# Reordering the middle of a streaming-encoder step and its routing list

## The chip, the cores and the metric

The kernel runs on one core of one Trainium2 chip. The metric is the device time of one execution, in microseconds (us); the median of several runs is quoted. PE is the matrix engine, DVE the vector engine, ACT the scalar engine, POOL the general one, SP the engine that only issues DMAs.

## The reference, cut to what matters

One layer is applied to a prompt of 512 tokens and to a sample of 64 tokens with a past of 512. In the kernel they are five row tiles: t = 0 to 3 of 128 rows, and t = 4 of 64.

```
z = rmsnorm(x) @ w_in                       # G, R, U, K, V, Q column blocks
o_gla, S = gla_recurrence(q, k, v, log_a, s0)     # 4 heads, chunks of 64
o_pool   = pool_mixer(u, hist)              # windows 2, 4, 8, 16
o_diff   = softmax(q0 k0') v - lam * softmax(q1 k1') v    # 4 heads, two maps
x += concat(o_gla, o_pool, o_diff) @ w_out
x += memory_attend(rmsnorm(x), mk, mv)      # mk, mv = rmsnorm(mem) @ w_mem_kv
x += sum over the 2 chosen of 16 experts of gate * (silu(h w_g) * (h w_u)) w_d
y  = rmsnorm(x)
```

## The kernel before, in words

**Order.** Each engine has its own instruction list, written out by hand, and engines meet only at semaphores. PSUM banks are handed out by plans: `PJ` (from `projection_plan`, two banks for projections), `TR` (transposes, two banks) and `SC` (scores, two halves). A plan gives each use its rank, its reader (A for ACT, V for DVE) and its bank; `claim` makes PE wait until the bank's previous user has been read.

**Split products.** Projections are in single precision made of two rounded parts. A weight unit of 128x2048 is loaded by SP (`dense_load`) into a ring of four (`DRING`), rounded by ACT (`w_high`) and its rest formed by DVE (`w_low`); a unit with a norm gain takes four instructions of 512 columns on each, a w_out unit one. A projection of a full tile with K = 1024 is 24 matmuls of 512 columns (hi*hi, lo*hi, hi*lo); of tile 4, whose two parts are packed, 16. Units 8, 9 are V, 10, 11 Q, 12, 13 memk, 14, 15 memv, 16 to 19 w_out. A load into a slot waits until tile 4 (or memory tile 1) of the unit four places back is projected.

**The middle.** PE projects blocks G, R, U, K and all five tiles of V, turns the decayed keys (`kend`), forms the chunk states (`kv`), projects Q0 and Q1, and runs five gated-attention tiles (`gla_scores`, `gla_out`), after which it projects Q2, Q3, Q4, memk0 and memk1 in turn; the pool products (`pool_map`) stand behind tiles 3 and 4. Then come the 20 steps s of differential attention (tile t = s // 4, head h = s % 4): PE does scores of step s + 1, waits for `pd_ready` of s, transposes the probabilities, and multiplies them by V. DVE forms row maxima (`row_max`) and normalises; ACT does the exponentials (`exps`). A filler stands in each step: a half (12 matmuls) of memv0 or memv1 in tile 0, of w_out of tile t - 1 afterwards. POOL splits units 16 and 17.

**Routing.** Behind the memory stage the x2 rows are transposed, `router` gives logits, DVE picks groups and experts (L1733 to L1757), `("pos",)` counts positions, and `placed` (one-hot of position) times `held` (entry by expert) gives the list `idx_sb` (L1784). Then DVE works out the overflow list (L1788 to L1810), and splits the first expert's gate weights (`split_lo(0, 0, 0)` and `(0, 0, 1)`). POOL gathers rows by the list (L741). Sixteen experts follow; in the last one DVE's order is `split_lo`, `hidden`, `hid_lo`.

## Time and profile before

| what | us |
|---|---|
| runs (3) | 838.66, 848.07, 848.48; median 848.07 |
| the profiled execution | 847.1 |
| its span, first to last instruction | 845.4 |
| mean granted PE clock over the span | 0.914 |

The profiled execution stands 1.0 us below the median and 1.7 us above its own span. Clock is in shares of full speed; a matmul row's duration overlaps its neighbours', so rates are read from the starts. [idle <-releaser] behind a row is the time that the engine stood before it and whose instruction ended that.

### The profile page before, as it was taken

The page shows a single profiled execution, that of the slowest core. Times are in us where ns is not written, and L with a number is a line of the kernel's source. Part 1 is how long each engine was busy: PE and PEld are TensorE (multiplying, and loading weights), DVE is VectorE, ACT ScalarE, POOL GpSimd, SP SyncE. Part 2 cuts the span into 40 slices and gives each one's busy share as a digit, 9 for nine tenths or more (in the row PEclk, how much of TensorE's full clock was granted, in tenths as well). Part 3 has the DMA queues.
Part 4 walks back from the last instruction along what each step waited for, and adds up shares of the span by engine and source line. Part 5 has one row for each costly group of instructions (what it writes and reads, how often), then busy time and mean ns, then how long its engine had stood idle before and what let it go on. Part 6 is the DMA issues. An engine that isn't in the chain of part 4 may idle for free.

```text
span 845.4 us, 9688 instructions
## 1 busy us (share of the span) xinstructions
PE 722.8 (86%) x3454; PEld 574.9 (68%) x3454; DVE 526.2 (62%) x660; ACT 416.5 (49%) x584; POOL 153.3 (18%) x171
## 2 busy tenths in 40 slices
PE   4979988998688898978898956999999999999920
PEld 3778876775465656657786854888888888888720
DVE  4533624563635445535644565898888898988817
ACT  5445433233233323333532322877788778788612
POOL 4102910011700101000001011121112321112004
PEclk9999999999599889889998756999999999999975
DMA  9323133123352000013005154899999999999346
GB/s 335 121 90 124 76 130 143 54 99 112 125 221 104 0 1 1 1 50 125 1 26 224 34 228 146 336 358 373 388 375 380 391 377 381 382 387 385 147 159 215
DMA packets 31631, 160.67 MB, mean 190 GB/s; under 512 B 5598, under 2 KB 5932, under 8 KB 16748
## 3 DMA queue, kind: packets, MB, share of 16 engines
q1 hardware_dynamic: 22224, 138.20, 42.8%
q10 hardware_dynamic: 4604, 12.26, 4.0%
q0 software_dynamic: 4768, 9.73, 3.1%
q8 instruction: 22, 0.36, 0.2%
q14 instruction: 13, 0.11, 0.0%
HBM read 150.90 MB, written 16.62 MB: 198 GB/s over the span
## 4 chain that ended last, share of the span: by engine, by line
PE 63%; DVE 15%; issue 10%; ACT 9%; DMA 3%; ACTq 0%; POOL 0%; SPq 0%; DVEq 0%; POOLq 0%
PE pj L1898 40%; PE scores L1898 15%; ACT wh L810 3%; PE tr_a L1906 3%; PE tr_v L1898 2%; DVE wl L1292 2%; PE tr_v L1906 1%; DVE w_lo L1320 1%; PE tr_a L2274 1%; DMA raw<-in_dense 1%; DVE hid L1292 1%; DMA yg<-y_rows 1%; DVE w_lo L1292 1%; ACT y L1217 1%; PE scores L2251 1%
## 5 line engine op out<-in xcount | busy, mean ns | idle before, releaser
L1292 DVE TENSOR_TENSOR wl<-moe_raw,wh 128x2048 fp32r<-128x2048 f32 x96 | 217.5, 2289 | 40.9 <-ACT wh L810 40.7
L810 ACT ACTIVATE wh<-moe_raw 128x2048 fp32r<-128x2048 f32 x96 | 182.4, 1920 | 35.6 <-PE scores L1898 12.0
L1898 PE MATMUL pj<-w_hi,xT_hi 128*128 128x512 f32 (+2 forms) x192 | 72.2, 376 | 11.7 <-DVE w_lo L1320 10.4
L685 POOL TENSOR_SCALAR rs<-stat 128x1 f32<-128x1 f32 (+4 forms) x31 | 11.4, 369 | 387.5 <-ACT sq_scr L823 202.0
L1898 PE MATMUL pj<-w_hi,xT_lo 128*128 128x512 f32 (+2 forms) x192 | 70.2, 365 | 0.0
L1898 PE MATMUL pj<-w_lo,xT_hi 128*128 128x512 f32 (+2 forms) x192 | 70.1, 365 | 0.0
L1320 DVE SCALAR_TENSOR_TENSOR w_lo<-raw,pack_a,w_hi 128x512 fp32r<-128x512 f32 (+2 forms) x64 | 44.8, 760 | 36.9 <-ACT w_hi L855 36.9
L746 POOL DMA_INDIRECT y_rows<-y,idx_sb x16 | 16.1, 1004 | 235.9 <-ACT y L1217 235.9
L1898 PE MATMUL pj<-wh,xgh 128*128 128x512 f32 x128 | 52.2, 408 | 2.8 <-DVE xgl L1292 2.8
L870 ACT ACTIVATE pdT<-tr_a 128x256 f32<-128x256 f32 (+4 forms) x24 | 9.4, 392 | 86.7 <-PE tr_a L1906 86.7
L1898 PE MATMUL scores<-wh,hTh 128*128 128x512 f32 x128 | 49.9, 390 | 1.4 <-DVE hTl L1292 1.4
L1898 PE MATMUL tr_v<-wh,xgh 128*128 128x512 f32 x128 | 51.1, 399 | 0.0
L1898 PE MATMUL pj<-wh,xgl 128*128 128x512 f32 x128 | 50.5, 394 | 0.0
L1898 PE MATMUL pj<-wl,xgh 128*128 128x512 f32 x128 | 50.4, 394 | 0.0
L1898 PEld LDWEIGHTS pj<-w_hi,xT_hi 128*128 128x128 f32 x192 | 37.7, 196 | 18.3 <-POOL ext L669 9.0
L1898 PE MATMUL tr_v<-wh,xgl 128*128 128x512 f32 x128 | 49.9, 390 | 0.0
L1898 PE MATMUL tr_v<-wl,xgh 128*128 128x512 f32 x128 | 49.9, 390 | 0.0
L1898 PE MATMUL scores<-wh,hTl 128*128 128x512 f32 x128 | 49.9, 390 | 0.0
L1898 PE MATMUL scores<-wl,hTh 128*128 128x512 f32 x128 | 49.8, 389 | 0.0
L741 POOL DMA_INDIRECT xg<-h_rows,idx_sb x16 | 41.7, 2604 | 16.3 <-DVE idx_sb L1784 7.5
L1898 PEld LDWEIGHTS pj<-w_hi,xT_lo 128*128 128x128 f32 x192 | 37.7, 196 | 5.5
L866 ACT ACTIVATE rowbuf<-pj,rs 128x512 f32<-128x512 f32 (+1 forms) x22 | 13.4, 607 | 56.9 <-PE pj L1898 56.9
(366 smaller groups left out, 1597.9 us busy)
## 6 DMA issues: line engine op xcount, KB each, us to landing
moe_raw<-in_w_exp_gate SPq DMA_DIRECT2D x32, 1024.0 KB, 7.3
moe_raw<-in_w_exp_up SPq DMA_DIRECT2D x32, 1024.0 KB, 7.3
moe_raw<-in_w_exp_down SPq DMA_DIRECT2D x32, 1024.0 KB, 8.2
raw<-in_dense SPq DMA_DIRECT2D x17, 1024.0 KB, 6.9
yg<-y_rows SPq DMA_DIRECT2D x4, 1024.0 KB, 9.4
xT_raw<-in_xT SPq DMA_DIRECT2D x4, 512.0 KB, 11.7
x_rows<-in_x_prompt SPq DMA_DIRECT2D x4, 512.0 KB, 12.3
xw<-in_x_prompt ACTq DMA_DIRECT2D x1, 2048.0 KB, 8.3
```

The source lines that it names most:

```text
L685: link(pool.tensor_scalar(rs[rows, n, cs], stat[rows, n, cs], EPS, None, ALU.add))
L741: pool.indirect_dma_start(xg[:, b, :], None, h3_rows, bass.IndirectOffsetOnAxis(ap=idx, axis=0), bounds_check=TOK - 1, oob_is_err=False).t ...
L746: pool.indirect_dma_start(y_rows, bass.IndirectOffsetOnAxis(ap=idx, axis=0), y[:, b, :], None, bounds_check=2 * TOK - 1, oob_is_err=False) ...
L810: act.activation(wh[s4][:, :], moe_raw[:, SLOT_OF[s6], :], ACT.Copy).then_inc(hi_done, 1)
L866: return act.activation(dst, src, ACT.Copy, scale=scale)
L870: act.activation(dst, src, ACT.Copy).then_inc(tr_act, 1)
L1217: act.activation(y[:, b, 512 * c:512 * c + 512], py[c], ACT.Copy).then_inc(y_done, 1)
L1292: return dve.tensor_tensor(out, a, b, op)
L1320: dve.scalar_tensor_tensor(out=w_lo[:, n % DRING, w * k:w * k + w], in0=srcs[k], scalar=gains[:, GAIN_OF[name], r // P + k:r // P + k + 1] ...
L1898: return pe.matmul(out, lhsT, rhs, start=start, stop=stop, skip_group_check=True)
L1906: ins = pe.transpose(bank[0:n, c0:c0 + r], src, ident[0:r, 0:r])
L2251: ins = pe.transpose(px[g][:, P * k:P * k + P], xg[:, buf, P * (4 * g + k):P * (4 * g + k) + P], ident[:, :])
```

## The change

In the middle only V0 is projected ahead of `kend`, V1 after `kv`, and V2, V3, V4, Q0 and Q1 stand behind the gated-attention tiles. Q2, Q3, Q4, memk0, memk1, memv0, memv1, three pool products and the four w_out projections of tiles 0 and 1 become fillers of steps 0 to 11, each split into a part ahead of the wait for `pd_ready` and a part behind the transposes. Projections that are fillers all use bank 1 and `diff_o` always bank 0. Splits of units 13 to 19 stand in steps 0 and 3 to 8 (`LATE_SPLIT`), all on ACT and DVE; POOL splits nothing. The memory transpose's split is in step 1. ACT does `exps` of the next step directly behind the copy of the transposes. For the list, `held` and `placed` are bf16 (four values of small size for each entry instead of two), the splits of the first expert's units stand elsewhere, the overflow list is worked out ahead of the last expert, `x2_T(4)` is ahead of `router(3)`, and one more Silu of one element stands behind the routing exponentials. In the diff eight columns of deep indentation are left off.

```diff
 def projection_plan():
-    plan = [((b, t), row_reader(t)) for b, _, _ in IN_BLOCKS[:-1] for t in range(TILES)] + [(("Q", t), "A") for t in range(2)]
+    plan = [((b, t), row_reader(t)) for b, _, _ in IN_BLOCKS[:-2] for t in range(TILES)] + [(("V", t), "A") for t in range(2)]
     for t in range(TILES):
         plan += [(("gla_o", t), "V")]
-        plan += [(("Q", t + 2), row_reader(t + 2))] if t + 2 < TILES else [(("memk", t - 3), "A")]
-        plan += [(key, "V") for key in POOL_USES[2 * t - 6:2 * t - 4]] if t >= 3 else []
-    for t in range(TILES):
-        plan += [(("w_out", c, t - 1), "V", 1 - t % 2) for c in range(2)] if t else [(("memv", i), "A", 1) for i in range(2)]
-        plan += [(("diff_o", t), "V", t % 2)]
+        plan += [(("V", t + 2), row_reader(t + 2))] if t + 2 < TILES else [(("Q", t - 3), "A")]
+    plan += [(("Q", t), row_reader(t), 1) for t in range(2, TILES)] + [(("memk", 0), "A", 1), (("diff_o", 0), "V", 0)]
+    plan += [(("memk", 1), "A", 1), (("memv", 0), "A", 1), (("memv", 1), "A", 1)]
+    plan += [(key, "V", 1) for key in POOL_USES[0:3]] + [(("diff_o", 1), "V", 0), (POOL_USES[3], "V", 1)]
+    for t in range(2, TILES):
+        plan += [(("w_out", c, u), "V", 1) for u in ((0, 1) if t == 2 else (t - 1,)) for c in range(2)]
...
 HIGH = {key: n for n, key in enumerate(high_plan())}
...
-WO_SPLIT = (5, 6)
+LATE_SPLIT = {0: 13, 3: 14, 4: 15, 5: 16, 6: 17, 7: 18, 8: 19}
...
-    sp.wait_ge(pj_full, PJ[("Q", 1)][0] + 1)
...
     sp.wait_ge(states_ready, 1)
...
+    for n in range(MK_UNIT, MV_UNIT):
+        dense_load(n)
+    sp.wait_ge(pj_full, PJ[("Q", 1)][0] + 1)
+    sp.dma_start(memT_raw[:, :, :], A["memT"]).then_inc(memT_in, 16)
     for n in range(MV_UNIT, MQ_UNIT):
         dense_load(n)
     sp.dma_start(mq_raw0[:, :], unit(MQ_UNIT)).then_inc(mq_in[0], 16)
...
     for t in range(TILES):
         root(("gla", t))
-    for n in (WO_UNIT, WO_UNIT + 1):
-        pool.wait_ge(unit_in[n % DRING], 16 * (n // DRING + (n % DRING > 0)))
...
-            c = slice(512 * k, 512 * k + 512)
-            link(pool.tensor_copy(w_hi[:, n % DRING, c], raw[:, n % DRING, c]))
-            pool.tensor_tensor(w_lo[:, n % DRING, c], raw[:, n % DRING, c], w_hi[:, n % DRING, c].bitcast(F32),
-                               ALU.subtract).then_inc(wo_done, 1)
...
-            act.activation(memT_hi[:, :, :], memT_raw[:, :, :], ACT.Copy).then_inc(memT_hi_done, 1)
         if t + 2 < TILES:
-            rows_block("Q", t + 2, ROW_AT[("Q", t + 2)])
...
+        if t == 4:
+            kq_out("Q", 0)
+        if t >= 3:
+            rows_block("Q", t - 3, ROW_AT[("Q", t - 3)])
         if t:
             mixg_high(t - 1)
-        if t >= 3:
-            mem_out("memk", t - 3)
-            for n in range(2 * t - 6, 2 * t - 4):
-                pool_high(n)
-        if t == 4:
-            mk_out(0)
-            w_high(MV_UNIT)
+    w_high(MK_UNIT)
...
+            exps(s + 1)
+        if s < 2:
+            rows_block("Q", s + 2, ROW_AT[("Q", s + 2)])
+        if s in (3, 4):
+            mem_out("memk", s - 3)
...
+        if s in (5, 6):
+            mem_out("memv", s - 5)
+        if s == 6:
+            pool_high(0)
+        if s == 7:
+            pool_high(1)
+            pool_high(2)
         if h == 1 and t:
             mixd_high(t - 1)
-        if s + 1 < len(STEPS):
-            exps(s + 1)
         if s == 0:
-            w_high(MV_UNIT + 1)
             act.wait_ge(state_out, 16 * 8)
             act.dma_start(xw[:, 0:4, :], A["x_prompt"][0].rearrange("(t p) n -> p t n", p=P)).then_inc(x_again, 16)
             act.dma_start(xw[0:DEC, 4, :], A["x_sample"][0]).then_inc(x_again, 16)
-        if t == 0 and h % 2 == 1:
-            mem_out("memv", h // 2)
-        if s in WO_SPLIT:
-            w_high(WO_UNIT + 2 + WO_SPLIT.index(s))
-        if h == 1 and t >= 2:
-            x1_square(t - 2)
+        if s == 1:
+            act.wait_ge(memT_in, 16)
+            act.activation(memT_hi[:, :, :], memT_raw[:, :, :], ACT.Copy).then_inc(memT_hi_done, 1)
+        if s in LATE_SPLIT and s != 7:
+            w_high(LATE_SPLIT[s])
         if h == HEADS - 1:
             act.wait_ge(pj_full, PJ[("diff_o", t)][0] + 1)
             act.wait_ge(ms_dve, TILES + t)
...
+            if t >= 2:
+                x1_square(t - 2)
+        if s == 7:
+            pool_high(3)
+            w_high(LATE_SPLIT[s])
...
     for i, v in enumerate((r20[1], r5[3])):
         act.wait_ge(route_arg, i + 1)
         act.activation(v, v, ACT.Exp).then_inc(route_exp, 1)
+    act.activation(small[0:1, 1:2], neghalf[0:1, 0:1], ACT.Silu)
...
     mixg_low(TILES - 1)
+    w_low(MK_UNIT)
     for s, (t, h) in enumerate(STEPS):
         r, nk, b = ROWS[t], keys_of(t), s % 2
+        if s == 9:
+            dve.wait_ge(x_again, 32)
+        if 9 <= s <= 12:
+            add_rows("w_out", (s - 9) % 2, (s - 9) // 2, xw, xw)
         sc_read(dve, last_score(t, h))
         link(dve.reciprocal(recip[0:r, b, :], psum_[0:r, b, :]))
         link(tt(recip[0:r, b, 1:2], recip[0:r, b, 1:2], lams[0:r, 5:6], ALU.mult))
         link(dve.tensor_scalar(prob[0:r, b, 1, 0:nk], prob[0:r, b, 1, 0:nk], recip[0:r, b, 1:2], None, ALU.mult))
...
             row_max(s + 1)
-        if s == 0:
-            w_low(MV_UNIT + 1)
+        if s == 1:
+            dve.wait_ge(memT_hi_done, 1)
+            tt(memT_lo[:, :, :], memT_raw[:, :, :], memT_hi[:, :, :].bitcast(F32), ALU.subtract)\
+                .then_inc(memT_lo_done, 1)
+        if s == 2:
+            fold_rows("Q")
+        if s == 6:
+            pool_low(0)
+        if s == 7:
+            pool_low(1)
+            pool_low(2)
         if h == 1 and t:
             mixd_low(t - 1)
-        if s in WO_SPLIT:
-            w_low(WO_UNIT + 2 + WO_SPLIT.index(s))
         if h == 0 and t:
             diff_norm(t - 1)
+        if s in LATE_SPLIT and s != 7:
+            w_low(LATE_SPLIT[s])
         if h == HEADS - 1:
-            if t:
...
     link(dve.tensor_reduce(r5[4], r20[1], AX.X, ALU.add))
     link(dve.reciprocal(r5[4], r5[4]))
...
-        link(dve.scalar_tensor_tensor(out=more, in0=cnt, scalar=float(P * q), in1=more, op0=ALU.is_gt, op1=ALU.add))
-    link(dve.memset(ones16, 1.0))
-    link(dve.tensor_tensor_scan(upto, ones16, more, 0.0, ALU.mult, ALU.add))
...
+    link(dve.tensor_scalar(listed, parts[:, 0], -64.0, float(EMPTY), ALU.mult, ALU.add))
+    tt(idx_sb[:, :, :].rearrange("p e v -> p v e"), listed, parts[:, 1], ALU.subtract).then_inc(pj_dve, 1)
+    split_lo(0, 0, 0)
+    split_lo(0, 0, 1)
     def x_lo(e, b):
         for g in range(2):
...
+    link(dve.tensor_scalar(more, cnt, float(P), None, ALU.is_gt))
+    for q in range(2, 5):
+        link(dve.scalar_tensor_tensor(out=more, in0=cnt, scalar=float(P * q), in1=more, op0=ALU.is_gt, op1=ALU.add))
+    link(dve.memset(ones16, 1.0))
+    link(dve.tensor_tensor_scan(upto, ones16, more, 0.0, ALU.mult, ALU.add))
...
+    link(dve.tensor_reduce(extra_f, r8x16, AX.X, ALU.add))
+    link(dve.tensor_copy(extra_i[:, 0:MAX_EXTRA], extra_f))
+    dve.tensor_copy(extra_i[:, MAX_EXTRA:MAX_EXTRA + 1], upto[0:1, E - 1:E]).then_inc(list_ready, 1)
     step(E - 1, 1, last=True)
     dve.wait_ge(list_ready, 1)
...
-            rows_T("Q", t + 1, 4)
-        else:
-            mk_T(0)
+            value(t + 2)
+        if t == 3:
+            query(0)
+        if t == 4:
+            rows_T("Q", 0, 4)
+            query(1)
+            tr_read(pe, ("K", 4))
+            tr_read(pe, ("Q", 0))
+            diff_scores(0)
         if t:
...
-            pe.wait_ge(poolw_in, 16)
-        if t >= 3:
-            for n in range(2 * t - 6, 2 * t - 4):
-                pool_map(n)
     mixg_T(TILES - 1)
-    tr_read(pe, ("K", 4))
-    tr_read(pe, ("Q", 4))
+    rows_T("Q", 1, 4)
     pj_read(pe, ("V", 3))
     pj_read(pe, ("V", 4))
-    mk_T(1)
+    def filler(s, part):
+        if s < 3:
+            query(s + 2, part)
+        elif s < 5:
+            mem_kv("memk", s - 3, part)
+        elif s < 7:
+            mem_kv("memv", s - 5, part)
+        elif s == 7:
+            pool_map(1 + part)
+        elif s < 12:
+            w_out((s - 8) % 2, (s - 8) // 2, part)
     for s, (t, h) in enumerate(STEPS):
         r, nb, b = ROWS[t], key_blocks(t), s % 2
         if s + 1 < len(STEPS):
+            if h == HEADS - 1:
+                tr_read(pe, ("Q", t + 1))
             diff_scores(s + 1)
+        if late_rows(s):
+            kind, i = late_rows(s)
+            rows_T(kind, i, 4) if kind == "Q" else mk_T(i)
+        filler(s, 0)
         pe.wait_ge(pd_ready, s + 1)
...
             transposes(("pd", t, h, 1), [(0, prob[0:r, b, 0, PAST:PAST + DEC])])
+        filler(s, 1)
         if h == 1 and t:
             mixd_T(t - 1)
-        if h >= 2:
-            if t:
-                w_out(1, t - 1, h - 2)
-            else:
-                mem_kv("memv", 1, h - 2)
+        if h >= 2 and t >= 3:
+            w_out(1, t - 1, h - 2)
         if h == 0:
             j = claim("pj", PJ, PJ_KEYS, ("diff_o", t), pj_act, pj_dve)
         tr_read(pe, ("pd", t, h, 0))
...
-        if h < 2:
-            if t:
-                w_out(0, t - 1, h)
-            else:
-                mem_kv("memv", 0, h)
+        if s == 6:
+            pe.wait_ge(pool_ready, 4)
+            pe.wait_ge(poolw_in, 16)
+            pool_map(0)
+        if s == 7:
+            pool_map(3)
+        if h < 2 and t >= 3:
+            w_out(0, t - 1, h)
     w_out(0, TILES - 1, 0)
     def x1_T(t):
...
     x2_T(TILES - 2)
     router(2)
+    x2_T(TILES - 1)
     router(3)
-    x2_T(TILES - 1)
     router(4)
...
-            ins = mm(pj[j][:, 0:2 * E], placed[0:r, i, t, :], held[0:r, i, t].rearrange("p v e -> p (v e)"),
+            ins = mm(pj[j][:, 0:4 * E], placed[0:r, i, t, :], held[0:r, i, t].rearrange("p v e -> p (v e)"),
                      i == 0 and t == 0, i == 1 and t == TILES - 1)
```

## Rows read from the trace of the kernel before
**Rows 1.** The page, part 1: busy time of each engine.
```profile
PE 722.8 (86%) x3454; PEld 574.9 (68%) x3454; DVE 526.2 (62%) x660; ACT 416.5 (49%) x584; POOL 153.3 (18%) x171
```
**Rows 2.** Windows: stretch, busy us by engine, PEclk, DMA share, GB/s.
```profile
209.00:242.00 33.00, 23.81 (x86) 17.16 (x85) 19.08 (x33) 11.03 (x35) 17.53 (x16) 0.74 0.33 116
215.90:306.90 91.00, 78.19 (x299) 53.41 (x299) 45.51 (x91) 28.45 (x75) 16.63 (x19) 0.86 0.27 101
```
**Rows 3.** PE timeline: start us, us, what, idle before and its releaser.
```profile
215.42 0.48 PE L1906 MATMUL tr_a<-ident,prob 128*128 128x128 f32 x1 [5.52 <-DVE prob L1593]
217.78 0.63 PE L1898 MATMUL pj<-w_hi,memT_lo 128*128 128x512 f32 x1
218.20 0.63 PE L1898 MATMUL pj<-w_hi,memT_hi 128*128 128x512 f32 x1
...
234.33 0.39 PE L1898 MATMUL pj<-w_hi,memT_hi 128*128 128x512 f32 x1
234.56 0.40 PE L1898 MATMUL pj<-w_lo,memT_hi 128*128 128x512 f32 x1
...
306.30 0.65 PE L1906 MATMUL tr_a<-ident,prob 128*128 128x128 f32 x4 [0.62 <-DVE prob L1593]
```
**Rows 4.** DVE timeline of the gated-attention preparation.
```profile
117.06 1.42 DVE L1292 TENSOR_TENSOR t<-t,gk 128x576 f32<-128x576 f32 x2
...
145.24 1.22 DVE L1292 TENSOR_TENSOR S<-scores,own 128x1024 f32<-128x1024 f32 x1 [2.21 <-PE scores L1898]
...
152.77 0.49 DVE L1466 SCALAR_TENSOR_TENSOR Ss<-Ss,dec_end 128x256 f32<-128x256 f32 x1
...
165.31 2.73 DVE L1320 SCALAR_TENSOR_TENSOR w_lo<-raw,pack_a,w_hi 128x512 fp32r<-128x512 f32 x4
```
**Rows 5.** ACT timeline: a gain split, exponentials, a row evacuation, a plain split.
```profile
162.46 2.55 ACT L855 ACTIVATE w_hi<-raw,pack_a 128x512 fp32r<-128x512 f32 x4
...
241.39 0.69 ACT L866 ACTIVATE mv<-pj,rs 128x512 f32<-128x512 f32 x1 [1.12 <-PE pj L1898]
...
245.92 0.47 ACT L1054 ACTIVATE prob<-scores,tiny 128x256 f32<-128x256 f32 x1
...
254.68 1.92 ACT L858 ACTIVATE w_hi<-raw 128x2048 fp32r<-128x2048 f32 x1
```
**Rows 6.** DVE timeline: the memory transpose's split.
```profile
182.51 2.28 DVE L1292 TENSOR_TENSOR memT_lo<-memT_raw,memT_hi 128x2048 fp32r<-128x2048 f32 x1
```
**Rows 7.** DVE timeline: a gain split while POOL splits weights.
```profile
218.08 4.68 DVE L1320 SCALAR_TENSOR_TENSOR w_lo<-raw,pack_a,w_hi 128x512 fp32r<-128x512 f32 x4 [1.49 <-ACT w_hi L855]
```
**Rows 8.** DVE timeline from the last memory projection to the expert loop.
```profile
481.84 2.29 DVE L1292 TENSOR_TENSOR wl<-moe_raw,wh 128x2048 fp32r<-128x2048 f32 x1 [1.09 <-ACT wh L810]
...
494.73 0.23 DVE L1642 SCALAR_TENSOR_TENSOR lg<-pj,rs,pack_a 64x20 f32<-64x20 f32 x1 [0.72 <-PE pj L1898]
...
503.79 1.07 DVE L1771 TENSOR_SCALAR scratch<-lane,scratch 128x128 f32<-128x128 f32 x5
...
508.44 0.19 DVE L1784 TENSOR_SCALAR idx_sb<-pj 128x32 int32<-128x32 f32 x1 [2.45 <-PE pj L1898]
...
513.02 4.47 DVE L1292 TENSOR_TENSOR wl<-moe_raw,wh 128x2048 fp32r<-128x2048 f32 x2
```
**Rows 9.** PE timeline of routing: the entries' products, the gathered rows, the first expert.
```profile
503.48 4.86 PE L1898 MATMUL pj<-scratch 128*128 128x32 f32 x20 [2.55 <-DVE scratch L1771]
513.94 1.97 PE L2251 MATMUL scores<-ident,xg 128*128 128x128 f32 x8 [5.61 <-DMA xg<-h_rows,idx_sb]
518.75 0.79 PE L1898 MATMUL pj<-wh,xgh 128*128 128x512 f32 x1 [2.83 <-DVE xgl L1292]
```
**Rows 10.** ACT timeline, first expert.
```profile
525.33 1.28 ACT L1203 ACT_TABLE_LOAD   x1
```
**Rows 11.** DVE timeline of the last expert.
```profile
798.14 2.29 DVE L1292 TENSOR_TENSOR wl<-moe_raw,wh 128x2048 fp32r<-128x2048 f32 x1 [0.97 <-ACT wh L810]
801.08 0.69 DVE L1292 TENSOR_TENSOR hid<-act_g,tr_v 128x512 f32<-128x512 f32 x1 [0.65 <-PE tr_v L1898]
```

More of the change, by code:

```diff
@@ L134, in high_plan @@
 def high_plan():
[L136 to L139 removed]
+    plan = [("mix_g", t) for t in range(TILES)] + [("mix_d", 0)] + POOL_USES + [("mix_d", t) for t in range(1, TILES - 1)]
     plan += [("x1", 0, g) for g in range(2)] + [("mix_d", TILES - 1)] + [("x1", 1, g) for g in range(2)]
@@ L158 @@
 PJ, TR, SC = numbered(projection_plan()), numbered(transpose_plan()), numbered(score_plan())
+for _a in (("diff_o", 1),):
+    (_i, _, _ra, _x), (_j, _w, _rb, _y) = PJ[_a], PJ[POOL_USES[3]]
+    PJ[_a], PJ[POOL_USES[3]] = (_i, _w, _rb, _x), (_j, _w, _ra, _y)
 HIGH = {key: n for n, key in enumerate(high_plan())}
@@ L546, in _ @@
             sp.dma_start(mem_rows[:, :, :], A["mem_prompt"][0].rearrange("(t p) n -> p t n", p=P)).then_inc(mem_in, 16)
-            for n in range(DRING, MK_UNIT + 2):
+            for n in range(DRING, MK_UNIT):
                 dense_load(n)
-            sp.wait_ge(pj_full, PJ[("Q", 1)][0] + 1)
-            sp.dma_start(memT_raw[:, :, :], A["memT"]).then_inc(memT_in, 16)
             sp.wait_ge(states_ready, 1)
@@ L657, in _ @@
             link(pool.iota(lane[:, :], [[1, P]], base=0, channel_multiplier=0, allow_small_or_imprecise_dtypes=True))
-            link(pool.tensor_copy(entry[:, :, :, :], tokid[:, :, :, :]))
-            link(pool.tensor_scalar(entry[:, :, :, :], entry[:, :, :, :], -float(EMPTY), None, ALU.add))
+            for v in range(2):
+                link(pool.iota(entry[:, :, :, 0, v], [[-TOK // 64 * v, 2], [-2, TILES]], base=30, channel_multiplier=0,
+                               allow_small_or_imprecise_dtypes=True))
+                link(pool.iota(entry[:, :, :, 1, v], [[0, 2], [0, TILES]], base=127, channel_multiplier=-1,
+                               allow_small_or_imprecise_dtypes=True))
             ready(pool.memset(empty[:, :], EMPTY))
@@ L996, in _, with value_rows @@
             act.activation(lams[:, 2:4], lams[:, 0:2], ACT.Exp).then_inc(lam_exp, 1)
-            for t in range(TILES):
-                if t in (2, 3):
-                    w_high(8 + t)
+            def value_rows(t):
                 if t < 4:
@@ L1005, in _ @@
                 act.dma_start(out.rearrange("m h d -> m (h d)"), vrow[0:ROWS[t], t, :]).then_inc(stored, 16)
-            for t in range(2):
-                rows_block("Q", t, ROW_AT[("Q", t)])
-            kq_out("Q", 0)
+            value_rows(0)
+            w_high(10)
+            value_rows(1)
+            w_high(11)
             def mixg_high(t):
@@ L1181, in _ @@
             h3_out_of(TILES - 1)
-            split_hi(0, 0, 0)
-            split_hi(0, 0, 1)
+            for j in (-1, 0, 1):
+                split_hi(0, 0, j)
             for i, v in enumerate((r20[1], r5[3])):
@@ L1471, in _ @@
                     ins.then_inc(states_ready, 1)
+            w_low(10)
             def mask_scores(t):
@@ L1854, in _ @@
             step(E - 2, 0)
+            link(dve.tensor_scalar(more, cnt, float(P), None, ALU.is_gt))
[3 more added lines that the diff above has]
+            link(dve.tensor_tensor_scan(upto, ones16, more, 0.0, ALU.mult, ALU.add))
+            link(tt(base, upto, more, ALU.subtract))
+            link(dve.tensor_scalar(base, base, float(P), -float(P + EMPTY), ALU.mult, ALU.add))
+            link(tt(r80[3], pos, base.unsqueeze(1).to_broadcast([P, TILES, E]), ALU.add))
+            link(dve.scalar_tensor_tensor(out=r80[0], in0=pos, scalar=P - 0.5, in1=r80[3], op0=ALU.is_gt, op1=ALU.mult))
+            for i in (1, 2):
+                link(tt(r80[i], r80[i], r80[0], ALU.mult))
+                link(dve.tensor_reduce(r5[6], r80[i], AX.X, ALU.add))
+                ins = dve.tensor_scalar(slot_i[:, i - 1, :], r5[6], float(EMPTY), None, ALU.add)
+                if i == 1:
+                    link(ins)
+            ins.then_inc(slots_ready, 1)
+            link(tt(r8x16, upto[0:1, :].unsqueeze(1).to_broadcast([1, MAX_EXTRA, E]),
+                    eidx[0:1, 0:MAX_EXTRA].unsqueeze(2).to_broadcast([1, MAX_EXTRA, E]), ALU.is_le))
+            link(dve.tensor_reduce(extra_f, r8x16, AX.X, ALU.add))
+            link(dve.tensor_copy(extra_i[:, 0:MAX_EXTRA], extra_f))
+            dve.tensor_copy(extra_i[:, MAX_EXTRA:MAX_EXTRA + 1], upto[0:1, E - 1:E]).then_inc(list_ready, 1)
             step(E - 1, 1, last=True)
```

137 lines of the change are left out of this document (44 added, 93 removed).

## The prediction

> **What bounds the kernel now.** I read the busy times first: PE is busy 86% of the span [rows 1], so the kernel is near PE's work, and what can be won is PE's idle time and the time that it runs at the lower of its two clock levels. PE's timeline then shows both rates: two neighbouring 512-column matmuls start 0.42 us apart at 1.2 GHz and 0.23 us apart at 2.4 GHz [rows 3]; a half projection (12 matmuls) is 2.73 us or 5.1 us. The windows tell where the loss lies: from step 0's transposes to step 12's, 91.0 us, PE is busy 78.2 us, and the mean clock of 0.86 means 0.14 x 2 x 91.0 = 25.5 us at the lower level [rows 2]. So 12.8 us are idle, half of 25.5 (12.7) is lost to the clock, and 65.7 us are work at the full rate. The first step is the worst: 5.52 us ahead of its transposes [rows 3], with a clock of 0.74 in the 33 us around it [rows 2]. The expert loop is PE's own; it moves as a block.
>
> **Part 1, up to step 0's transposes.** Moved behind that point: Q3, Q4, memk0, memk1 and half of Q2 (2 x 2.73 for each full one, 3.6 for Q4, 2.7 for the half: 22.7 us), their transposes (some 2 us) and the pool products (some 1.2 us), 25.9 us. Undisturbed, step 0's transposes would go from 215.9 to 190.0.
> V0 ends at 118.6. The decayed keys are ready at 118.5 (the end of the row at 117.06) [rows 4], so `kend` needn't wait, though the four V tiles that covered it are gone. With two short waits for the copies `kv` runs from 120.5 to 124.7, V1 to 130.2. Now the cover is gone: the chunk states are ready 153.3 - 143.1 = 10.2 us behind `kv`'s start (2.15 us ahead of the row at 145.24) [rows 4], thus at 130.7; behind them DVE does `w_low(10)`, 2.7 us [rows 4], and a head product of 0.65, and only then may PE score tile 0, at 134.1. PE waits 3.9 us where Q0 and Q1 stood before (bounds: 0, if V1 ran at the lower level and covered it, and 10.2 - 4.2 + 2.7 = 8.7 with nothing to cover the chain). I take it to fall to the lower level, as it did around the wait of 5.52, for some 6.6 us, +3.0. The five tiles follow at PE's pace with V2 to V4, Q0, Q1: it is at step 0 at 177.3. There ACT must do `w_high(12)`, 2.55 us [rows 5], and only then exponentials (0.9); DVE `w_low(12)`, 2.7, behind a copy that comes after them, then 1.0 of normalising. Transposes end at 185.4, 4.6 us better than the 190.0. PE waits 3.8 us there (before 5.5), and falls again.
>
> **Part 2, steps 0 to 11.** Per step there are two paths from one step's transposes (T) to the next. PE's: second half filler 2.73, product with V 0.4 to 0.95, scores 1.1 to 2.4, a transpose of 0.45 where one stands there, first half 2.73, T 0.25 to 0.45. The engines' round: the filler full at T + 2.73, its evacuation 0.7 [rows 5] and an output DMA 0.4 (T + 3.9), the unit's `w_high` 2.55 or 1.92 [rows 5], `w_low` 0.7 behind it for a gain unit (pipelined by fours) or 2.29 for a w_out unit (the same shape as the split at 481.84 [rows 8]), normalising 0.95 to 1.2, T. The exponentials (two of 0.47 and their sums [rows 5], 1.05) lie in the 2.73 that ACT waits for the filler. Step by step, PE path / round, and what I take:
> s0 7.7 / 8.3, and 2.4 for the low level, 10.7. s1 6.75 / 9.0 (memory split 1.9 on ACT, 2.28 on DVE [rows 6]), 9.0; the wait of 2.3 brings a fall. s2 7.0 + 3.2 = 10.2. s3 8.3 / 9.4. s4 8.55 / 8.75. s5 8.55 / 10.3 (two kinds of split behind `mixd`). s6 6.5 / 10.35. s7 6.4 / 11.0: it has only pool products for PE, four pool evacuations in one bank, `diff_sq` and unit 18 in a row. s8 8.8 / 9.8. s9 and s10 9.3, PE's. s11 6.55 / 7.6.
> The sum is 115.7 us (PE alone 93.7). Step 12's transposes end at 185.4 + 115.7 = 301.1; before, 306.95 (the row at 306.30 [rows 3]). Gain 5.85. The projections find nothing to hide but one another: 22 of the idle and slow microseconds are still there, since each step now carries a split and an evacuation that the loops before it used to carry.
> POOL's splits fall away. While they ran, four chunks of a gain split took DVE 4.68 us [rows 7] against 2.73 [rows 4]; I use 2.73 throughout. Loads: a unit is asked for when the tile-4 use four places back is full, two steps ahead of its split, 14 to 16 us, and lands in 5 to 8; I cost them at nothing; late, each would add its lateness to one step.
> (The Trainium skill, SBUF — State Buffer, in "SBUF: two separate sides", says that the port pair of DVE and POOL is an exclusive lock for the whole instruction, against DVE operations with two SBUF inputs. By it the 1.95 us difference would be gone for each of the two splits; the sum above has it gone too. The trace's 4.68 against 2.73 agrees.)
>
> **Part 3, diff_o in one bank.** At steps 12 and 16 no filler stands behind the transposes, and the product with V must now wait until `diff_norm` has read the old `diff_o`: 0.5 and 0.3 us more. +0.8.
>
> **Part 4, routing.** The split at 481.84 (2.29) [rows 8] stood ahead of the additions of tile 4; without it they start at 484.1 for the second half and only two are left, and `x2_T(4)` comes 2 us earlier. The last logits go from 494.73 [rows 8] to 491.7: -3.0. `held` is twice as wide, +0.35. Entries: 20 matmuls of 4.86 us [rows 9] become 10 in bf16; bounds 0 and 4.86 us, the present length, as no row has this shape; I take 0.6, since each takes one pass over 64 columns instead of two over 32, and little but the start is left. But DVE does the moved split (2.29) and 1.2 of gates behind the last `placed` (503.79 + 1.07 [rows 8]), so the list is ready 3.9 us behind it, as before (508.63): the faster products are hidden by the split. Behind the list only 4.47 us of splits stand, not 4.5 of overflow list and 4.47 more [rows 8]; then the gathered rows are last (513.94 [rows 9]): two transposes, ACT, DVE, 3.3 us. PE starts at 518.2 less the tail's gain instead of 518.75 [rows 9]: -0.5 with a bit for the gather's sharing with a 1 MB load. The table load of 1.28 us [rows 10] leaves the path, but Silu waits for PE until 0.75 ahead of its present start: -0.75.
> (The Trainium skill, ScalarE: Activation LUTs, "What ACT_TABLE_LOAD costs", gives about 1.3 us and a drain of 1.4 for every switch. By its 2.7 the edit would still win no more than PE's 0.75. The trace shows the load 0.02 us behind the split ahead of it, with no drain.)
>
> **Part 5, the last expert.** The overflow list, 4.54 us of DVE, now stands ahead of the split at 798.14. DVE has 0.97 and 0.65 us free around it [rows 11], so `hidden` and all behind it come 4.54 - 1.62 = 2.9 us later: +2.85. PE then stands 3.6 us instead of 0.8. Cost of a fall there: between 0 and 2.7 (half of the 24 last matmuls); I take 2.0.
>
> **Sum.** -5.85 + 0.8 - 3.0 - 0.5 - 0.75 + 2.85 + 2.0 = -4.45. From the profiled 847.1: 842.7 us. Against the median of 848.07 that is 0.6% less. A measurement of this kernel tells some 2% from no change (831 to 865).
>
> **Rivals.**
> A, PE-bound steps (0.2): the clock holds through the waits, and rounds run shorter than I add them. For it: in the trace waits of about 1 us left the rate alone. Then T12 is at 182.4 + 93.7 + 8 = 284.1, 17 us under my 301.1, and the last fall is away too: 842.7 - 17 - 2 = 824; with half of that effect 833.
> B, slower (0.15): the low level feeds itself. At 1.2 GHz the filler is full 2.4 us later, this lengthens the round by the same, the wait stays, and the level never comes back in steps 0 to 8. Nine times 2.4 is 21.6, of which 5.6 is in my sum: +16, 858.7. For it: in the first 33 us of the steps the clock was 0.74 [rows 2] with just such waits. Against: behind them PE recovered. It decides when the wait in each step is over some 2 us; I add 0.2 to 4.
> C, the last expert's list is free (0.2): the splits of expert 15 are ahead far enough, or PE's stand is short: 842.7 - 4.85 = 837.9.
> The forecast itself has 0.45 (838 to 848).
>
> **How the numbers follow.** The range takes C, half of A and most of B: 828 to 856. Of A's 0.2 half lies under 831, with a little of C: faster 0.11. Slower by over 2% (over 865) needs B and a late load: 0.03. Within: 0.86.
>
> **What would show it.** Right: PE idle near 4 us ahead of the first gated scores, released through `q_heads` by DVE; step 0's transposes near 185; step 12's near 301; s7 the longest step; the list's release to gather about as late behind `placed` as before; no ACT_TABLE_LOAD ahead of the first Silu; DVE 4.5 us of small operations at the end of expert 14 and `hid` 2.9 us later. Wrong: steps of 8 us with no waits (A), a clock under 0.7 over steps 0 to 8 (B), waits of ACT's `w_hi` on the DMA, or T12 later than 307.

## The result, and the profile after

The changed kernel takes 858.41 us (median of 4 runs, 856.37 to 860.40) against 843.42 for the kernel before beside it (4 runs, 838.66 to 848.48): ratio 1.0178, 95% interval 1.0116 to 1.0241. It is slower, by 1.2 to 2.4%, where I had forecast 842.7 and 828 to 856. With more runs the median of the kernel before is 847.4 to 847.8 (13 to 25 runs, 835.9 to 854.8). Executions of it fall into two groups, 836 to 840 us and 845 to 855, so medians over all runs move with how many of each there are, while each ratio leaves out the runs more than 1.5% above its kernel's fastest. Where the two differ, the text gives both. One profile of each kernel says little about 5 us; I therefore compare stretches inside the profiles.

The profiled execution of the changed kernel took 860.25 us, its span 858.6. The page's busy line, to be held against [rows 1]:
```profile
PE 725.2 (84%) x3444; PEld 574.1 (67%) x3444; DVE 523.7 (61%) x663; ACT 420.3 (49%) x587; POOL 136.2 (16%) x157
```
PE is busy for 2.4 us more with nearly the same work, in a span 13.2 us longer: 10.8 us more idle. POOL lost its splits. The windows from step 0's transposes to step 12's, and from there to the first transposes of `x1`:
```profile
190.07:309.24 119.17, 102.36 (x426) 72.16 (x424) 54.80 (x107) 45.24 (x99) 4.15 (x7) 0.91 0.31 117
309.24:374.49 65.25, 55.18 (x264) 38.77 (x265) 29.03 (x54) 19.57 (x48) 3.91 (x7) 0.90 0.01 2
```
In [rows 2] PE stood idle for 12.8 us and lost 12.7 to the clock. Now it is 16.8 (119.17 - 102.36) and, at a clock of 0.91, 0.09 x 2 x 119.17 = 21.5 us at the lower level, half of it (10.7) lost. The work at the full rate is 119.2 - 16.8 - 10.7 = 91.7 us, as it should be: 65.7 before and the 25.9 that were moved in. But idle and clock together cost 27.5 us where they cost 25.5: the moved projections filled none of the idle time. The clock rose from 0.86 to 0.91, and PE's idle share of the steps is 14% both times. PE's timeline shows the waits, one line for each place (compare [rows 3, 9]; last comes the idle time before, and what ended it):
```profile
136.64 1.19 PE L1911 MATMUL scores<-gq,t 128*128 128x512 f32 x1 [3.39 <-DVE gq L1298]
...
199.21 0.33 PE L1919 MATMUL tr_a<-ident,prob 128*128 128x128 f32 x1 [1.33 <-DVE prob L1595]
208.25 0.33 PE L1919 MATMUL tr_a<-ident,prob 128*128 128x128 f32 x1 [2.23 <-DVE prob L1595]
...
257.54 0.44 PE L1919 MATMUL tr_a<-ident,prob 128*128 128x128 f32 x2 [3.15 <-DVE prob L1595]
261.24 0.69 PE L1911 MATMUL pj<-ext,poolw 128*128 128x64 f32 x2 [3.27 <-DVE plT_lo L1528]
...
309.24 0.68 PE L1919 MATMUL tr_a<-ident,prob 128*128 128x128 f32 x4 [1.22 <-DVE prob L1595]
311.18 2.07 PE L1911 MATMUL pj<-vrow,pdT 128*128 128x128 f32 x8 [1.26 <-DVE mixd L1298]
...
324.26 0.50 PE L1911 MATMUL pj<-w_hi,mdT_hi 128*128 128x512 f32 x1 [1.85 <-DVE mdT_lo L1298]
...
523.71 1.97 PE L2275 MATMUL scores<-ident,xg 128*128 128x128 f32 x8 [11.43 <-DMA xg<-h_rows,idx_sb]
527.10 0.80 PE L1911 MATMUL pj<-wh,xgh 128*128 128x512 f32 x1 [1.41 <-DVE xgl L1298]
...
812.91 1.12 PE L2298 MATMUL tr_a<-ident,hid 128*128 128x128 f32 x4 [3.50 <-DVE hid L1298]
815.44 0.79 PE L1911 MATMUL scores<-wh,hTh 128*128 128x512 f32 x1 [1.41 <-DVE hTl L1298]
```
Transposes of single steps wait 0.65 to 3.15 us for `prob` (steps 1, 2, 4, 5, 6 and 7). What VectorE does ahead of `prob` in step 1 (its timeline):
```profile
195.44 2.74 DVE L1326 SCALAR_TENSOR_TENSOR w_lo<-raw,pack_a,w_hi 128x512 fp32r<-128x512 f32 x4 [5.87 <-ACT w_hi L854]
198.09 0.16 DVE L1592 RECIPROCAL tiny<-tiny 128x2 f32<-128x2 f32 x1
...
198.80 0.35 DVE L1595 SCALAR_TENSOR_TENSOR prob<-prob,tiny 128x128 f32<-128x128 f32 x1
```
ScalarE's exponentials for this step were done at 191.5. VectorE then stood idle for 5.87 us, for the split of a unit that PE needs first in step 3, and the normalising that PE needs now stands behind it.

Five profiles by stretch, from one milestone's start to the next (m_only and a_list have the middle as changed, r_only as before; m_only has the routing as before):

| stretch, us | before | after | m_only | r_only | a_list |
|---|---|---|---|---|---|
| step 0's transposes at | 215.42 | 190.07 | 190.44 | 214.60 | 184.40 |
| to step 12's | 90.88 | 119.17 | 119.07 | 87.43 | 114.74 |
| to `x1`'s first | 61.01 | 65.25 | 65.32 | 57.15 | 65.36 |
| to last logits | 127.42 | 126.72 | 126.98 | 124.82 | 126.06 |
| to `idx_sb` | 13.71 | 14.06 | 13.71 | 14.06 | 14.05 |
| to first expert product | 10.31 | 11.83 | 10.30 | 11.91 | 11.91 |
| to last `hid` | 282.33 | 285.09 | 283.42 | 284.61 | 282.85 |

a_list is, up to the experts, the changed kernel itself; it reached step 12 at 299.14, the changed kernel at 309.24 and m_only at 309.51. Ten microseconds there are the execution's, not the code's.

### The profile page after: what moved, and what is told of

Same layout as the page of the kernel before. It is cut to its first block, busy times and chain, and to the rows that moved or that the text cites. A ratio compares the mean times of both kernels' runs of the same rounds, so it can differ in the third digit from the quotient of the medians.

```text
span 858.6 us, 9664 instructions
## 1 busy us (share of the span) xinstructions
PE 725.2 (84%) x3444; PEld 574.1 (67%) x3444; DVE 523.7 (61%) x663; ACT 420.3 (49%) x587; POOL 136.2 (16%) x157
## 4 chain that ended last, share of the span: by engine, by line
PE 72%; DVE 13%; ACT 5%; issue 4%; DMA 3%; POOL 1%; SPq 0%; ACTq 0%; DVEq 0%; POOLq 0%
PE pj L1911 43%; PE scores L1911 15%; PE tr_v L1911 8%; PE tr_a L1919 2%; PE scores L2275 2%; PE tr_v L1919 2%; DVE w_lo L1326 2%; PE tr_a L2298 1%; DMA raw<-in_dense 1%; DMA yg<-y_rows 1%; DVE w_lo L1298 1%; ACT w_hi L854 1%; DVE wl L1298 1%; DMA xg<-h_rows,idx_sb 1%; POOL rs L694 1%
## 5 line engine op out<-in xcount | busy, mean ns | idle before, releaser
L1911 PE MATMUL pj<-w_hi,xT_hi 128*128 128x512 f32 (+2 forms) x192 | 75.7, 394 | 11.1 <-DVE w_lo L1326 11.1
L1911 PE MATMUL pj<-w_lo,xT_hi 128*128 128x512 f32 (+2 forms) x192 | 73.0, 380 | 0.0
L1911 PE MATMUL pj<-w_hi,xT_lo 128*128 128x512 f32 (+2 forms) x192 | 72.7, 379 | 0.0
L1326 DVE SCALAR_TENSOR_TENSOR w_lo<-raw,pack_a,w_hi 128x512 fp32r<-128x512 f32 (+2 forms) x64 | 42.2, 720 | 41.9 <-ACT w_hi L854 41.8
L1911 PEld LDWEIGHTS pj<-w_hi,xT_hi 128*128 128x128 f32 x192 | 39.9, 208 | 18.3 <-POOL keep L673 8.7
L1911 PEld LDWEIGHTS pj<-w_hi,xT_lo 128*128 128x128 f32 x192 | 39.7, 207 | 6.1
L1911 PEld LDWEIGHTS pj<-w_lo,xT_hi 128*128 128x128 f32 x192 | 39.8, 208 | 5.0
## 6 DMA issues: line engine op xcount, KB each, us to landing
x_rows<-in_x_prompt SPq DMA_DIRECT2D x4, 512.0 KB, 12.1
```

The costliest lines, as they stand in the source:

```text
L1326: dve.scalar_tensor_tensor(out=w_lo[:, n % DRING, w * k:w * k + w], in0=srcs[k], scalar=gains[:, GAIN_OF[name], r // P + k:r // P + k + 1] ...
L1911: return pe.matmul(out, lhsT, rhs, start=start, stop=stop, skip_group_check=True)
```

## The experiments

**r_only.** The kernel before with the routing part alone (entries in bf16, the moved splits, the routers' order, the early Silu, the overflow list behind expert 14).

> The kernel before with only the routing part of the change: bf16 entries, the moved splits, router order, early Silu table, overflow list behind expert 14. Theory (the two profiles added up): the tail wins about 2, the gather's rows come 2 to 3 later, the last expert's list costs 2.7 and its down products at the lower clock 1.4, so +3 to +6 us against the kernel before. Rival (my prediction's terms, -3.0 -0.5 -0.75 +4.85): +0.6 us, and then the middle carries the whole +15. In the profile the theory wants an idle of 2 to 4 us ahead of the last expert's hid transposes and none over 1.5 in its middle.

853.28 us against 847.39: ratio 1.0131 (1.0034 to 1.0228), +5.9. The idle ahead of the last `hid` transposes is 3.49. By the ratio it is 1.3%, some 11 us. The theory holds. The routing part alone makes the kernel slower; how much of the loss is its own the medians don't tell.

**m_only.** The kernel before with the reordered middle alone.

> The kernel before with only the middle reordered, routing as before. Theory: up to step 12 no gain (-0.6), steps 12 to 20 lose 4.3, so +3 to +5 us; if the 3.5 us by which the changed kernel stood late at V0 belong to the change and not to the run, +7 to +9. Rival (my prediction): -5 us. The profile should show ahead of step 13's block of mixd products a wait for mdT_lo near 1.9 us and ahead of steps 12's and 16's products with V one for mixd of 1.3.

854.74 us, ratio 1.0128 (1.0032 to 1.0225), +7.3. By the medians over all runs the halves cost 5.9 and 7.3 us and the two together 11.0; by the ratios 1.3% each and 1.8% together. The changed kernel stands 5.1 above r_only and 3.7 above m_only. So each half loses something and neither carries it all; their shares, and whether they add, lie inside the intervals. The 3.5 us by which the changed kernel stood late at V0 are the execution's, since a_list had them back with the same code.

**a_norm.** The changed kernel, each split of VectorE one place later:
```diff
                 if s + 1 < len(STEPS):
                     row_max(s + 1)
-                if s == 1:
+                if s - 1 in LATE_SPLIT:
+                    w_low(LATE_SPLIT[s - 1])
+                if s == 2:
...
-                if s in LATE_SPLIT and s != 7:
-                    w_low(LATE_SPLIT[s])
...
-                    w_low(LATE_SPLIT[s])
```
(The split under `s == 1`, now `s == 2`, is the memory transpose's.)

> The changed kernel, but each step's w_low on VectorE stands behind the next step's normalising (the memory split too). Theory: the round that sets steps 0 to 8 is filler, evacuation, both halves of the split and only then normalising; with the split behind, the waits of 1.33, 2.23, 1.49, 0.65, 1.84 and 3.15 us ahead of the transposes of steps 1 to 7 go, and most of the lower clock they brought: -8 to -12 us against the changed kernel, step 12's transposes near 299. Rival 1 (the low clock feeds itself whatever the waits): under 3 us, waits gone but clock still near 0.8. Rival 2 (ScalarE's w_high is the round): waits shrink by the 2.3 to 2.7 of VectorE only where ScalarE isn't last, -4 us.

846.33 us, 12.1 less than the changed kernel's 858.41. The window of steps 0 to 11:
```profile
189.66:294.35 104.69, 97.07 (x426) 68.63 (x424) 55.01 (x107) 45.26 (x99) 4.16 (x7) 0.97 0.35 133
```
104.7 us, where the seven profiles with these splits as changed have 114.7 to 119.5; the clock is 0.97. The waits for `prob` at steps 1, 2, 5, 6 and 7 are gone; that of step 4 is 1.16. So both rivals fall: once the waits went the clock rose too, and with VectorE's half moved and ScalarE's left in place more than 10 us went. One thing stayed:
```profile
250.09 0.43 PE L1910 MATMUL pj<-ext,poolw 128*128 128x64 f32 x2 [3.46 <-DVE plT_lo L1528]
```
Step 7's pool products share a bank, and the read of the second stands behind exponentials on ScalarE and now a split on VectorE. And 2 us came back behind step 12 (67.4 us to `x1`, where 65.3 stands for the others).

**a_list.** The changed kernel, the overflow list in four pieces behind experts 0, 1, 14 and 15:
```diff
+            step(0, 0)
             link(dve.tensor_scalar(more, cnt, float(P), None, ALU.is_gt))
...
+            step(1, 1)
             link(tt(base, upto, more, ALU.subtract))
...
+            step(E - 2, 0)
             for i in (1, 2):
                 link(tt(r80[i], r80[i], r80[0], ALU.mult))
...
+            step(E - 1, 1, last=True)
             link(tt(r8x16, upto[0:1, :].unsqueeze(1).to_broadcast([1, MAX_EXTRA, E]),
```

> The changed kernel with the overflow list cut in four pieces, behind experts 0, 1, 14 and 15 (1.2, 0.9, 1.3 and 0.8 us). Theory: VectorE has 2.1 us to spare per expert, so the idle of 3.50 ahead of the last hid transposes falls to about 0.8 and the last down products keep the full clock (5.75 instead of 7.10): -3.5 to -4 us. Rival: the last expert's wait comes from another chain (Silu, the load of its last unit): no change.

853.21 us, -5.2 against the changed kernel's 858.41. PE's timeline of its last expert:
```profile
800.11 0.66 PE L2295 MATMUL tr_a<-ident,hid 128*128 128x128 f32 x4 [0.84 <-DVE hid L1298]
802.17 0.50 PE L1908 MATMUL scores<-wh,hTh 128*128 128x512 f32 x1 [1.41 <-DVE hTl L1298]
```
0.84 as before the change, instead of 3.50. From the first expert product to VectorE's first use of the gathered outputs it is 4.4 us less.

**a_steps12 and a_mixd.** The changed kernel with two edits taken back from tile 3 on, and with one of them:
```diff
-                if s + 1 < len(STEPS):
-                    exps(s + 1)
...
                 if h == 1 and t:
                     mixd_high(t - 1)
+                if s + 1 < len(STEPS):
+                    exps(s + 1)
...
-        plan += [(("diff_o", t), "V", 0)]
+        plan += [(("diff_o", t), "V", t % 2)]
```
(the second, with w_out in the other bank, only in a_steps12).

> The changed kernel, but from tile 3 on diff_o alternates its banks as before, and ScalarE reads mixd's transposes ahead of the next exponentials again. Theory: the waits of 1.26 and 1.42 us ahead of steps 12's and 16's products with V fall to about 0.3, those of 1.85 and 1.47 for mdT_lo at steps 13 and 17 to under 0.3, and from step 12's transposes to x1's first transposes it takes 61 us or less instead of 65.3: -4.3 us. Rival: the waits only move to the next row (the exponentials come 0.6 us later) and the stretch stays above 64 us.

> The changed kernel with mixd's transposes read ahead of the exponentials again, diff_o in one bank as changed. From step 12's transposes to x1's it takes 65.3 us in the changed kernel and 58.5 with both mendings. Theory: the waits of 1.85 and 1.47 for mdT_lo go, those of 1.26 and 1.42 for mixd stay; the stretch is near 61.5, since a wait here costs again by the lower clock behind it. Rival: the banks are the larger part, 63 or more.

a_steps12: 849.74 us, -8.7. a_mixd, a single run: 852.90. Their windows from step 12's transposes to `x1`'s, a_steps12's first:
```profile
304.35:362.81 58.46, 52.81 (x265) 37.05 (x265) 29.21 (x54) 19.46 (x48) 3.91 (x7) 0.94 0.01 2
```
```profile
306.66:368.20 61.54, 54.75 (x265) 38.48 (x266) 29.22 (x54) 19.36 (x48) 3.92 (x7) 0.89 0.01 4
```
65.25 in the changed kernel, 61.54, 58.46: the read of `mixd` behind the exponentials costs 3.7 us, the single bank 3.1. The sum is firm: the stretch takes 65.25 to 65.4 us in five of the six profiles with both edits as changed (67.4 in a_norm), and 58.5 to 59.6 in four with both taken back. How it divides rests on a_mixd's one run. The 3.7 are nearly all waits (1.85 and 1.47 are gone, the clock is 0.90 and 0.89); of the 3.1 only 1.1 are, and the rest comes with the clock's rise to 0.94. In a_mixd the first product with V of step 12 (308.60) still carries the wait for `mixd`, 1.28; in a_steps12 there is only one for `pdT`:
```profile
305.78 2.05 PE L1911 MATMUL pj<-vrow,pdT 128*128 128x128 f32 x8 [0.78 <-ACT pdT L869]
```
The wait for `mdT_lo` begins on ScalarE, here in the changed kernel:
```profile
321.48 0.69 ACT L1044 ACTIVATE prob<-scores,tiny 128x512 f32<-128x512 f32 x1 [0.28 <-DVE tiny L1558]
...
322.82 0.59 ACT L831 ACTIVATE mdT_hi<-tr_v 128x512 fp32r<-128x512 f32 x1
```
`mixd`'s transposes were done at 321.0; ScalarE came to them 1.8 us later, 1.3 of it exponentials, and PE stood until 324.26.

**a_early.** The changed kernel, unit 10's split in tile 0's turn and unit 11's in tile 1's:
```diff
                     ins.then_inc(states_ready, 1)
-            w_low(10)
...
-                if t == 0:
-                    w_low(11)
+                if t < 2:
+                    w_low(10 + t)
```

> The changed kernel, but unit 10's split by VectorE stands in tile 0's turn and unit 11's in tile 1's, not ahead of the first masked scores. Theory: the wait of 3.39 us ahead of the first gated scores falls by the 2.7 of the split, and step 0's transposes come 3 to 5 us earlier (wait, and half of what PE does behind it at 1.2 GHz). Rival: the wait ends later anyway by the chunk states (decay chain), -1 us or less; or the split is late for Q0's projection and the wait comes back there.

849.48 us, -8.9. The wait ahead of the gated scores:
```profile
136.24 1.10 PE L1910 MATMUL scores<-gq,t 128*128 128x512 f32 x2 [0.74 <-DVE gq L1298]
```
0.74 instead of 3.39, the 2.65 of a split. From `kv`'s first product to step 0's transposes it takes 59.2 us, in seven profiles of the order as changed 62.9 to 65.8. A wait of 1.77 then shows at step 0 and none at Q0.

**a_gather.** The changed kernel, the list first, then gates, then splits:
```diff
-            split_lo(0, 0, -1)
-            dve.wait_ge(route_exp, 1)
...
             dve.wait_ge(pj_full, PJ[("entries",)][0] + 1)
...
             tt(idx_sb[:, :, :].rearrange("p e v -> p v e"), listed, parts[:, 1], ALU.subtract).then_inc(pj_dve, 1)
+            dve.wait_ge(route_exp, 1)
...
+            split_lo(0, 0, -1)
             split_lo(0, 0, 0)
```

> The changed kernel, but idx_sb is made as soon as the entries are there, then the gates, then all three splits. From list to first expert product it took 10.3 us in the kernel before and in the one with the middle alone, 11.8 in all four with the routing part; the two gathers' issues on GpSimd took 1.22 and 1.01 us in the former and 2.39 and 1.70 in the latter. Theory: VectorE's splits (two operands from SBUF) hold GpSimd's descriptor writing up. Then the first issue, beside the gates' small operations, takes 1.2 us again, the second, beside a split, 1.7; the list is ready 3.3 us earlier behind placed, and the first product comes 3 to 4 us earlier behind the last logits. Rival: the loads of 1 MB issued at the same time slow the rows; then the issues stay at 2.4 and 1.7 whatever VectorE does.

849.29 us, -9.1. From the last logits to the first expert product it is 20.65 us instead of 25.89, so 5.2 of the 9.1 are seen there; the rest is in no stretch that the edit touches. GpSimd's issues in the changed kernel and SyncE's next loads, then the same of a_gather with VectorE's split:
```profile
516.37 2.38 POOL L740 DMA_INDIRECT xg<-h_rows,idx_sb  x1 [7.81 <-DVE idx_sb L1298]
519.05 1.69 POOL L740 DMA_INDIRECT xg<-h_rows,idx_sb  x1 [0.30 <-issue]
...
517.69 2.53 SPq L579 DMA_DIRECT2D moe_raw<-in_w_exp_up  x2
```
```profile
506.44 1.22 POOL L740 DMA_INDIRECT xg<-h_rows,idx_sb  x1 [5.07 <-DVE idx_sb L1298]
507.95 1.93 POOL L740 DMA_INDIRECT xg<-h_rows,idx_sb  x1 [0.30 <-issue]
...
506.71 4.50 DVE L1298 TENSOR_TENSOR wl<-moe_raw,wh 128x2048 fp32r<-128x2048 f32 x2
...
510.83 1.97 PE L2274 MATMUL scores<-ident,xg 128*128 128x128 f32 x8 [5.75 <-DMA xg<-h_rows,idx_sb]
...
511.23 2.53 SPq L579 DMA_DIRECT2D moe_raw<-in_w_exp_up  x2
```
The first issue takes 1.22 though a split begins 0.27 us behind its start; the second, which begins inside the split, takes 1.93. In the changed kernel the split was there a microsecond earlier (515.38), and the first took 2.38. All fourteen profiles agree: the first issue takes 1.21 or 1.22 in the seven where no split runs when it begins, and 2.38 or 2.39 in the seven where one does. What counts for the issue is which of the two begins first. The theory is right as far as that. But from the list to the rows' transposes 3.0 us were won (8.44 to 5.48), and the issues end only 0.9 sooner (5.47 behind `idx_sb`'s start, now 4.53). The other 2.1 lie between the issues' end and the rows. There SyncE's two 1 MB loads were issued at 517.69, ahead of the rows; here at 511.23, behind them. That is the rival's mechanism; no run holds one without the other, so how the 2.1 are shared stays open.

**a_all.** All of it in one, and in step 7 ScalarE reads the first pool product ahead of the transposes' copy and VectorE does unit 17's split behind the pool products.

> The changed kernel with all the mendings in one: unit 10's and 11's splits in tiles 0 and 1, each step's split behind the next step's normalising, step 7's pool products read first, mixd read ahead of the exponentials, diff_o's banks alternating from tile 3 on, the list and gather ahead of gates and splits, the overflow list in four pieces. Theory (the parts add): against the changed kernel -4 (start), -12 (steps), -3 (step 7), -4.3 (steps 12 to 20), -3.4 (gather), -4 (last expert), about -28 of 858, so 826 to 834 and faster than the kernel before by 1 to 2%. Rival (the clock takes back what waits give): half of it, 840 to 845.

820.40 us (817.68 to 823.58), ratio 0.970 (0.961 to 0.979): 38.0 less than the changed kernel, where 28 were expected, and 27 less than the kernel before by the medians over all runs, 3% or 25 us by the ratio. By their medians the five mendings sum to 44.0 us, more than the whole; by the stretches that they mend (6.6, 14.5, 6.8, 5.2 and 4.4 in the profiles) to 37.5, and a_all's profile is 37.8 shorter from K's last transposes to the gathered outputs' first use. So the parts add, and the medians of the single ones, against four runs of the changed kernel, are up to 4 us too large.

**m_mend and r_mend.** Which half carries this: the kernel before with the mended middle alone, and with the mended routing alone.

> The kernel before with the middle reordered and its mendings (early splits of units 10 and 11, splits behind the next normalising, step 7's pool products, mixd and the banks), routing as before. Theory: the reordering is worth much once no split stands in a step's round: x1's first transposes near 347 to 352 as in the version with all mendings, against 367 in the kernel before, so 826 to 833, 2% faster than the kernel before. Rival: most of the 27 us that the version with all mendings wins is routing; then 838 or more.

> The kernel before with the routing part and its two mendings (list and gather ahead of gates and splits, overflow list in four pieces), middle as before. Theory: 853.3 of the routing part alone less 5 for the gather and 4 for the last expert, 842 to 846, so within 1% of the kernel before and on its good side. Rival (middle is not where the gain lies): 835 or less.

828.09 us, ratio 0.9847 (0.9774 to 0.9921), and 841.48, ratio 0.9957 (0.9899 to 1.0015). By the medians over all runs (847.79 before) the mended middle wins 19.7 us and the routing 6.3; by the ratios 1.5% (13 us), and 0.4% (4 us) with no change inside its interval. The theory holds for the middle, with `x1`'s first transposes at 348.3; the routing's 841.48 lies just under its 842 to 846. Most of the gain is the middle's.

**a_all2.** On top of a_all, `diff_sq` ahead of step 3's `w_high`, and VectorE's split behind `diff_norm` in step 4.

> The version with all mendings, and diff_sq ahead of step 3's split on ScalarE, and step 4's split on VectorE behind diff_norm. Theory: the waits of 1.16 us ahead of step 4's transposes and of 0.84 ahead of its products with V go, and with them the lower clock of step 4 (11.0 us where its neighbours take 8.7 to 9.2): -3 us, 817 median. Rival: the next wait takes their place: no change.

818.55 us (816.20 to 820.92), ratio 0.9747 (0.9673 to 0.982). Step 4 takes 8.3 us instead of 11.0, and the steps' window is
```profile
184.58:284.90 100.32, 96.51 (x426) 68.66 (x424) 55.00 (x107) 45.02 (x99) 4.15 (x7) 0.97 0.37 139
```
against 103.55 in a_all. In the medians it is 1.9 us, which their spread doesn't tell from nothing. Of 100.3 us PE is busy 96.5: the steps are now PE's own, as rival A of the prediction had them, once the splits are out of the round.

## Why the prediction was wrong

**What bounds the kernel.** Right: PE's idle time and clock in the middle. From K's last transposes, ahead of everything that was changed, to `x1`'s first it is 254.8, 244.3 and 254.7 us in the three profiles with the old middle and 230.3 in a_all2, 14 to 24 less; the windows had shown 12.8 idle and 12.7 of clock to be lost in the steps.

**Part 1.** The wait ahead of the gated scores was forecast as 3.9 us, released through `q_heads` by VectorE: 3.39. The reason was right too, since 2.65 of it were `w_low(10)`. Step 0's transposes were forecast for 185.4; the seven profiles with this order give 184.4 to 190.4. The wait of 3.8 at step 0 wasn't there: PE reached it late, its last filler wholly or partly at half the rate (in a_early, where it ran at the full rate, 1.77 showed). Two errors that nearly cancel.

**Part 2.** The sum of the steps was 115.7, measured 114.7 to 119.5. That it is so near is luck in good part: step 0 took 9.1 instead of 10.7 and step 2 7.2 instead of 10.2, and steps 6, 7 and 8 took 13.0, 14.5 and 11.5 instead of 10.35, 11.0 and 9.8 (step 7 the longest, as forecast). The round (filler, evacuation, both halves of the split, normalising) is what a_norm shows to be the bound. Steps 1 and 3 to 5 are at their terms (9.0, 9.6, 9.2 and 10.4 against 9.0, 9.4, 8.75 and 10.3). In step 2 the low level that I had put there hadn't come. In step 7 four pool products in one bank, which I had counted as evacuations, cost PE a stand of 3.27 us, and then its scores ran at half rate. What failed is the gain drawn from it: "Step 12's transposes end at 301.1; before, 306.95". The one number is a sum, the other a single execution; r_only reached the place at 302.03 with the old middle. Over the profiles the new middle, its splits as changed, reaches step 12 at 305.8 in the mean (299.1 to 309.5, six of them: the changed kernel, m_only, a_list, a_gather, a_steps12, a_mixd) and the old one at 305.9 (302.0 to 309.5: before, r_only, r_mend). From K's last transposes on, which takes out what an execution lost earlier, it is 191.7 us with the new middle and 191.5 with the old. The 5.85 us weren't there.

**Part 3.** This is, with the 5.85 of Parts 1 and 2, the step that failed most: "+0.8" for `diff_o` in one bank. It measured 3.1 us: 1.1 of waits, near my 0.8, and 2.0 of clock, which isn't in the term. And `mixd_high` behind the exponentials, 3.7 us, isn't in the sum at all. The diff shows it as a line moved by a few places in ScalarE's order; I priced the reads that it adds to the steps and not the one that it delays.

**Part 4.** The tail, from `x1`'s first transposes to the last logits, gained 0.7 us in the changed kernel and 2.6 in r_only. Over all profiles it is 124.8 us in the eleven with the changed routing and 127.3 in the three without, 2.5 of my 3.0. The list came as late behind the last `placed` as before (3.6 us), the fast entries hidden by the split, as forecast. Wrong is "-0.5 with a bit for the gather's sharing": from list to first product it is +1.5. I had taken the gather's issue as fixed, and moved a split to where it starts; a_gather gives 0.9 us of that to the issue and leaves 2.1 open between it and the loads. The table load fell into idle time, as forecast.

(The Trainium skill, SBUF — State Buffer, in "Who interferes with whom", says that the order of issue decides which of VectorE and GpSimd blocks. For the issue the trace agrees, 1.22 us where it began first and 2.38 where it didn't. For VectorE it doesn't show it: the pair of splits that began behind an issue took 4.50 us, the pair that began ahead of one 4.49. I had used the page's lock for GpSimd's splits and not for its gather.)

**Part 5.** 2.85 + 2.0 forecast. From the first expert product to the last `hid` the seven profiles with the list behind expert 14 take 284.8 us in the mean and the seven others 282.7; from there to VectorE's first use of the gathered outputs 21.4 and 19.3. So 2.1 + 2.1: the sum of 4.2 is 0.65 short of the term, and rival C is out. The second part is a mean only: m_only has the first down product at the lower rate (0.79) behind a stand of 0.84.

**The rivals.** B gave the right time (858.7) for the wrong reason, by luck. Its sign, a clock under 0.7 over steps 0 to 8, wasn't there: the clock is 0.91 over steps 0 to 11. And the low clock doesn't keep itself up: in a_norm the waits went and the clock rose to 0.97 by itself. A was right of the kernel with the splits moved and wrong of this one. No rival had the true shape, small losses in five places, each of them an order on one engine or in the plan of banks. Nor did the range allow for terms of the sum that err to one side.

**The sum again.** Parts 1 and 2: -5.85 forecast, about 0 measured. Part 3: +0.8, and 6.8 with `mixd`. Part 4: -4.25, and -0.65 (-2.5, +0.35 for `held`, +1.5). Part 5: +4.85, and +4.2. That is -4.45 forecast and +10.4 measured, where the medians say +11.0 to +15.0.
